# Two-block model kernel: first weight block in columns, time-step product in column strips, first decays of the delta layer ahead of its gate, and that layer's end by halves of the heads

## The reference, cut to what matters

```python
# first block: SSD mixer, then a mixture of experts, then a norm
proj = rmsnorm(x, norm_mix) @ w_in            # 1024 x (z, xbc, dt, sc_b, sc_c, sc_v)
dt = softplus(dt_raw + dt_bias)               # dt_raw: 16 columns of proj
...
# second block: layers fox0, gla, gdn (the delta layer), fox1
q, k, v = split(silu(causal_conv(qkv, conv_w)))
gc = cumsum(g, per chunk of tokens)
decay = exp(gc[i] - gc[j]) where i >= j
tri = strict_lower((k*beta) @ k.T * decay) + eye
u, w = solve(tri, v*beta), solve(tri, k*beta*exp(gc))
# per chunk: v_new = u - w @ state; o = q_dec @ state + qk @ v_new
# state = state*dec + k_dec.T @ v_new
return (rms_norm(o) * silu(z)) @ w_out
```

## Time and profile before

| | |
|---|---|
| median of 3 runs | 1295.03 us (1293.96 to 1295.28) |
| the profiled execution's own time | 1292.94 us |
| its span in the trace | 1291.2 us |
| PE, DVE, ACT, POOL busy | 86%, 50%, 34%, 1% of the span |
| time-mean granted PE clock | 0.964 of full speed |

### The profile page before, as it was taken

One profiled execution on the slowest core, in us unless ns is written; L12 is line 12 of the kernel. 1 busy time (PEld: TensorE's weight loads), 2 busy tenths in 40 slices (PEclk: granted clock), 3 DMA queues, 4 the chain that ended last, 5 costly groups with the idle time before them and its releaser, 6 DMA issues.

```text
span 1291.2 us, 19652 instructions
## 1 busy us (share of the span) xinstructions
PE 1106.5 (86%) x8060; PEld 811.6 (63%) x8060; DVE 644.5 (50%) x1265; ACT 439.2 (34%) x691; POOL 8.0 (1%) x35
## 2 busy tenths in 40 slices
PE   8999899897676758585858999999999979899998
PEld 7999767543131314131414789887779869778897
DVE  6787578420101111020104767667567965656685
ACT  5554435100000000000003556536346653255563
POOL 1000000000000000000000000000000000000000
PEclk9999999999898989898989999999999989899999
DMA  8575345999999999999998974254324530056600
GB/s 299 144 260 196 131 157 196 398 409 409 409 409 410 409 410 410 410 409 410 410 410 296 289 223 155 106 196 143 118 94 168 183 79 4 1 130 172 235 19 33
DMA packets 120005, 314.66 MB, mean 244 GB/s; under 512 B 17139, under 2 KB 17386, under 8 KB 119674
## 3 DMA queue, kind: packets, MB, share of 16 engines
q1 hardware_dynamic: 116864, 310.78, 65.9%
q0 software_dynamic: 352, 2.11, 0.4%
q10 hardware_dynamic: 2714, 0.71, 0.3%
HBM read 312.52 MB, written 1.06 MB: 243 GB/s over the span
## 4 chain that ended last, share of the span: by engine, by line
PE 58%; DMA 28%; DVE 8%; ACT 3%; issue 2%; SPq 1%; DVEq 0%; ACTq 0%
DMA ring<-in_w_up 18%; DMA ring<-in_w_down 10%; PE bank L2250 7%; PE bank L2243 7%; PE bank L2247 7%; PE bank L2225 6%; PE bank L2229 6%; PE bank L2232 6%; PE bank L2540 3%; PE bank L2563 2%; DVE w_l L1202 1%; PE bank L2158 1%; DMA ring<-in_w_in 1%; PE bank L2646 1%; ACT w_h L673 1%
## 5 line engine op out<-in xcount | busy, mean ns | idle before, releaser
L1202 DVE TENSOR_TENSOR w_l<-ring,w_h 128x1024 fp32r<-128x1024 f32 x204 | 246.6, 1221 | 90.7 <-ACT w_h L673 89.0
L673 ACT ACTIVATE w_h<-ring 128x1024 fp32r<-128x1024 f32 x204 | 213.6, 1056 | 176.4 <-PE bank L2232 88.7
L2540 PE MATMUL bank<-ring,cm 128*32 128x512 f32 x880 | 137.1, 754 | 101.0 <-DMA ring<-in_w_gate 61.5
L2540 PEld LDWEIGHTS bank<-ring,cm 128*32 128x32 f32 x880 | 27.7, 124 | 208.6 <-issue 78.5
L2243 PE MATMUL bank<-w_h,hnT_h 128*128 128x512 f32 x480 | 135.6, 405 | 5.1 <-DVE cm L1829 1.9
L2250 PE MATMUL bank<-w_l,hnT_h 128*128 128x512 f32 x480 | 129.7, 392 | 5.5 <-DVE w_l L1202 5.5
L2247 PE MATMUL bank<-w_h,hnT_l 128*128 128x512 f32 x480 | 129.7, 392 | 0.0
L1676 DVE SCALAR_TENSOR_TENSOR cm<-cm,bank 128x512 f32<-128x512 f32 x8 | 5.5, 688 | 215.0 <-ACT cm L895 215.0
L2250 PEld LDWEIGHTS bank<-w_l,hnT_h 128*128 128x128 f32 x480 | 89.6, 188 | 27.4 <-DVE w_l L1202 8.5
L2247 PEld LDWEIGHTS bank<-w_h,hnT_l 128*128 128x128 f32 x480 | 90.6, 189 | 20.0 <-DVE hnT_l L1317 0.2
L2243 PEld LDWEIGHTS bank<-w_h,hnT_h 128*128 128x128 f32 x480 | 86.9, 190 | 25.2 <-issue 4.5
(11 more groups left out here) (442 smaller groups left out, 1354.9 us busy)
## 6 DMA issues: line engine op xcount, KB each, us to landing
ring<-in_w_down SPq DMA_DIRECT2D x62, 1024.0 KB, 15.9
ring<-in_w_gate SPq DMA_DIRECT2D x56, 1024.0 KB, 15.6
ring<-in_w_up SPq DMA_DIRECT2D x54, 1024.0 KB, 15.8
ring<-in_fox_w_in SPq DMA_DIRECT2D x32, 1024.0 KB, 11.3
ring<-in_w_in SPq DMA_DIRECT2D x22, 1024.0 KB, 9.6
ring<-in_gla_w_in SPq DMA_DIRECT2D x12, 1024.0 KB, 6.3
ring<-in_gdn_w_in SPq DMA_DIRECT2D x12, 1024.0 KB, 6.8
ring<-in_w_out SPq DMA_DIRECT2D x8, 1024.0 KB, 6.3
```

Of the source, the lines that this page charges most:

```text
L673: af(part(w_h, u, width), w, ACT.Copy).then_inc(s["high_ready"], 1)
L1202: v.tensor_tensor(part(w_l, u, width), w, part(w_h, u, width).bitcast(F32), ALU.subtract).then_inc(s["low_ready"], 1)
L2540: x = mm(bank[a][CAP * e:CAP * (e + 1), :], m_xg[:, 2 * b + r, CAP * e:CAP * (e + 1)], expert_of(w, e)[:, r * FF:(r + 1) * FF], start=(b = ...
```

## The change

- The first weight block is loaded as one DMA of columns 0 to 255 of all 1024 rows (1 MB, semaphore `columns_loaded`), then two DMAs for the other columns. Units 0 and 1 wait for the first alone.
- `norm_mix` is the first vector loaded, counts with x in `x_loaded`, and is transposed and copied by itself, ahead of x's transposes; the other vectors are transposed in `first_steps`, after unit 2. On ACT the squares of x stand after the high parts of units 0 and 1.
- The eight dt products go to four column strips of PE (two products in each), with the 16 weights doubled to 32 columns by a copy on POOL; DVE copies the four partial sums and one more product adds them, after unit 10 (`dt_parts`, `dt_sum`).
- In `gdn()` the first spread of gc goes to bank 3 and its product to bank 4, and stands on PE ahead of the last z unit. On ACT the first z block stands ahead of the last convolution's Silu, the two decays of chunk 0 ahead of the second z block and of that Silu, and three w_h units of the output weights are moved into the inversion. The same units' w_l move on DVE.
- The end of `gdn()` goes by halves of the heads on PE, DVE and ACT; PE gets 20 unread products between the first transposes, and units 0 and 1 of the output projection both stand ahead of the third transposes.

```diff
+            def put_first(w, col):
+                slot = slot_whole(0)
+                v = w[:, col:col + BLK].rearrange("(c p) n -> p c n", p=P)
+                sp.dma_start(slot[:, :, 0:2 * P], v[:, :, 0:2 * P]).then_inc(s["columns_loaded"], 16)
+                for h in (0, 1):
+                    sp.dma_start(slot[:, 4 * h:4 * h + 4, 2 * P:BLK], v[:, 4 * h:4 * h + 4, 2 * P:BLK]).then_inc(ready[0], 16)
...
+            pool.wait_ge(s["small_loaded"], 16 * N_EARLY)
+            nc.gpsimd.tensor_copy(w_dt[:, :, 1, :], w_dt[:, :, 0, :]).then_inc(s["consts_ready"], 1)
...
+                if k == 3:
+                    break
...
+                high(UNIT_BASE["gdn_out"] - 1)
                 token_z("gdn", 16, 0)
-                high(UNIT_BASE["gdn_out"] + PARTS - 1)
+                high(UNIT_BASE["gdn_out"])
                 act.wait_ge(s["gdn_col_step"], 1)
-                token_z("gdn", 16, 1)
                 af(tok[:, 4:6, 0:8], tok[:, 4:6, 0:8], ACT.Exp).then_inc(s["gdn_col_step"], 1)
-                high(UNIT_BASE["gdn_out"] + PARTS)
...
                 decay(0, 0)
                 decay(0, 1)
+                token_z("gdn", 16, 1)
+                act.wait_ge(s["lin_ready"], 3 + 4)
+                af(tf(12, 4), vtm[:, 0, :], ACT.Silu).then_inc(s["gdn_conv_done"], 1)
...
-            def small_full(dst, w):
+            def dt_parts():
 
                 for k in range(KD):
-                    x = mm(dst, w[:, k, :], hnT[:, k, :], start=(k == 0), stop=(k == KD - 1))
+                    strip = slice(32 * (k % 4), 32 * (k % 4) + 32)
+                    x = mm(bank[5][strip, 0:T], w_dt[:, k].rearrange("p a b -> p (a b)"), hnT[:, k, :],
+                           start=(k < 4), stop=(k >= 4), tile_position=(0, 32 * (k % 4)), skip_group_check=True)
                 x.then_inc(s["small_done"], 1)
+
+            def dt_sum():
+
+                pe.wait_ge(s["rows_step"], 1)
+                mm(bank[5][0:16, 0:T], every16[:], rows[:, 0], start=True, stop=True).then_inc(s["small_done"], 1)
...
+                def gdn_tail():
+
+                    out, gains = UNIT_BASE["gdn_out"], [VCOL["gdn_o_gain"]] * 2
+                    out_sums("gdn", 8, 0, (0,))
+                    held_keys(0)
+                    out_sums("gdn", 8, 0, (1,))
+                    out_roots(8, 0, 1.0 / P, None, (0,))
+                    held_keys(1)
+                    new_values(0)
+                    out_roots(8, 0, 1.0 / P, None, (1,))
+                    new_values(1)
+                    out_roots(8, 0, 1.0 / P, None, (2,))
+                    for p in (0, 1):
+                        out_gated(8, 16, 0, p)
+                    out_sums("gdn", 8, 1, (0,))
+                    out_roots(8, 1, 1.0 / P, slice(8, 12))
+                    for p in (0, 1):
+                        out_gated(8, 16, 1, p)
+                    turned_low("gdn", 0, gains)
+                    out_sums("gdn", 8, 1, (1,))
+                    turned_low("gdn", 1, gains)
+                    out_roots(8, 1, 1.0 / P, slice(12, 16))
+                    for p in (2, 3):
+                        for t in range(NT):
+                            out_gated(8, 16, t, p)
+                        turned_low("gdn", p, gains)
+                        low(out + PARTS + p - 2)
```

More of the change, by code:

```diff
@@ L251, in build @@
         heads = sb("heads", [P, 3, 2 * 16])
-        rows = sb("rows", [16, 4, T])
+        rows = sb("rows", [P, 4, T])
         fall = sb("fall", [P, T])
@@ L1120, in link, with inverse_root @@
                 dve.wait_ge(s["dve_chain"], n_link[0])
-            def inverse_root(dst, x, t, done=None):
-                link(v.tensor_scalar(dst.bitcast(I32), x.bitcast(I32), -0.5, RSQRT_SEED, ALU.mult, ALU.add))
-                for k in range(3):
+            def inverse_root(dst, x, t, done=None, rounds=range(3)):
+                if 0 in rounds:
+                    link(v.tensor_scalar(dst.bitcast(I32), x.bitcast(I32), -0.5, RSQRT_SEED, ALU.mult, ALU.add))
+                for k in rounds:
                     link(v.tensor_tensor(t, dst, dst, ALU.mult))
@@ L1256, in first_norm @@
                 dve.wait_ge(s["vec_turned"], 2)
+                v.tensor_copy(vec[:, KD:NA], bank[3][:, KD:NA])
                 link(v.tensor_copy(vec[:, P:P + NB], bank[3][:, P:P + NB]))
@@ L2771, in gdn, with falls, last_block @@
                 project("gdn", 4, 5, lambda m: m == 3 and turn_sums("gdn_qk"))
[L2772 to L2774 removed]
+                def falls(c, hf):
+                    for j in range(4):
+                        x = tr(b4(g_fall[c][hf])[:, j, :], tok[:, c, 4 * hf + j:4 * hf + j + 1].to_broadcast([P, P]), ident[:])
+                    x.then_inc(s["gdn_fall"], 1)
+                def last_block(m):
+                    if m in (1, 2):
+                        spread("gdn_qk", 8, lambda i: [2 * (i % 4) + i // 4], [2 * m - 2, 2 * m - 1])
+                    if m == 2:
+                        pe.wait_ge(s["proj_copied"], PROJ_BASE["gdn"] + 10)
+                        falls(0, 0)
+                project("gdn", 5, 6, last_block)
                 def turn_values(c, hf):
+                    pe.wait_ge(s["gdn_conv_done"], 3 + hf)
                     if c:
@@ L2793, in blocks @@
                     return a.rearrange("p (h d) -> p h d", d=P)
-                def falls(c, hf):
-                    for j in range(4):
-                        x = tr(b4(g_fall[hf])[:, j, :], tok[:, c, 4 * hf + j:4 * hf + j + 1].to_broadcast([P, P]), ident[:])
-                    x.then_inc(s["gdn_fall"], 1)
                 def products(c, hf):
```

193 lines of the change are left out of this document (110 added, 83 removed).

## The result

The changed kernel takes 1288.42 us (median of 5 runs, 1286.89 to 1290.37) against 1295.03 (1293.96 to 1295.38). The ratio is 0.995, with a 95% interval from 0.9937 to 0.9964: 6.6 us faster, where 13.5 were forecast. The time lies 0.1 us inside the slow end of the range (1281.5, range 1277.5 to 1288.5), which is no credit to the mechanism: the range was that wide for rivals that did not come as written. Its profiled execution took 1288.80 us (span 1287.1), 4.1 less than that of the kernel before. A join is the step behind the last power that binds the two 64x64 inverses of each head together; there is one for each of the two chunks.

A forecast was written before the change was run, and what follows sets the result against it. DMA was taken as busy throughout only in the experts; work saved ahead moves their stream, work saved behind moves the end. Gains 2.8+2.1+6.1+2.5 = 13.5 us gave a median of 1281.5, range 1277.5 to 1288.5.

The forecast's parts named there:

- the clock's share of the head: Delta layer's head: 0.6 us taken off 6.7 for one slow PE stretch possibly falling on the powers; lower bound 3.5.
- PEclk of 0.5 within the inversion: Sign that the forecast is wrong: PE at half clock within the delta layer's inversion; no size given.
- First block, 2.8: Kernel start: first 1 MB lands at 9.3, so the root's spread begins 2.8 us earlier; bounds 0 and 3.1.
- Time step, 2.1: dt products: four strips and an added sum replace 3.56 us of PE, saving 2.1; bounds loss 0.45, gain 2.3.
- That what the front saves moves the whole stream of the experts: Ahead of the experts: work saved lets their loads start earlier and moves their whole stream; 2.8 and 2.1 us.
- rival 2: Experts: their DMA-bound stream swallows what the front saves, only 8.6 us of gain remain, 1286.4 us; chance 8%.
- Head, 6.1: Delta layer's head: halves 7.1 us earlier, copy of the first power 6.1 earlier; bounds 3.5 and 7.1.
- End, 2.5: Delta layer's end: work by halves of heads starts the output projection's unit 3 2.5 us earlier; bounds 1 and 3.5.
- Rival 3: Delta head: each added table switch costs another 1.28, or slow stretch hits powers twice; 2.6 us, 1284.1; chance 15%.
- Rival 4: Delta layer: the inversion stays at 1.2 GHz, some 28 us more, 1309.5 us; chance 3%.

The follow-up runs named there:

- e5: The changed kernel itself, run again for a second trace: 1287.50 us, 0.9921 of the kernel before.
- e3: Kernel before with only the delta layer's head changed: 1291.14 us, 0.9964 of the kernel before.
- e7: Changed kernel plus unread products ahead of the experts (14 more at the start, 16 between the sums of squares, 6 before the gather): 1287.59 us, 0.9918 of before.
- e10: Changed kernel plus 5 unread products ahead of the first join and 5 ahead of the first corner: 1285.70 us, 0.9915 of the kernel before.
- e12: Changed kernel plus only 16 unread products between the two sums of squares at 133 us: 1288.28 us, 0.9939 of the kernel before.
- e6: Changed kernel plus unread products in the delta layer (20 before halves, 24 before second power, 5 before first join, 5 before first corner): 1283.38 us, 0.9895 of before.
- e1: Kernel before with only the first block's change: 1292.29 us, 0.9995 of the kernel before.
- e11: e6 (18 products, not 24) plus early table load, 16 products between the sums, and ACT's first w_h moved behind the second power's copies: 1281.32 us, 0.9881 of before.
- e8: Changed kernel plus the unread products of e6 and e7 and a small activation moving the first table load earlier: 1282.79 us, 0.9888 of the kernel before.
- e2: Kernel before with only the time step's four strips: 1294.08 us, 0.9998 of the kernel before.
- e13: e9 with its 38 unread products moved ahead of PE's wait for the convolution: 1292.28 us, 0.9969 of the kernel before.
- e9: Kernel before plus unread products in the delta layer (38 before first spread, 22 before halves, 8 before second power, 5 and 5 at joins): 1295.99 us, 1.0002.
- e14: e11 plus 17 unread products around the first transposes of the gated linear attention's output: 1282.82 us, 0.9900 of the kernel before.
- e4: Kernel before with only the delta layer's end changed: 1293.82 us, 0.9993 of the kernel before.

## Why the prediction was wrong, by its steps

**The step that failed** is the clock's share of the head: "I take off 0.6 because PE now pauses three times where it was slow anyway", with a lower bound of 3.5 for "the slow stretch on two steps", and a rival that priced half clock only as the whole inversion at 1.2 GHz. The runs put between them a middle that the text did not have: single stretches of about 1.5 us of loss, where PE has pauses or thin work, and at places that the account of the head never reached, since it ended at the copy of the first power. One of its own signs of being wrong came, "PEclk of 0.5 within the inversion". In the changed kernel's layer they cost 0.7 at the halves (in the changed kernel and e5; 0.2 or less in e3, e7, e10 and e12), 1.3 to 1.6 behind the 3.1 us pause ahead of the second power (in each of these six traces, all without unread products there: 34.1 to 34.4 us from the first power's copy to the first join's, against 32.8 to 32.9 with them), 1.8 at the joins and 1.7 behind them (in two of the five without products there). e6 takes all of it back. How much the joins matter shows between traces of the same layer: from the entry to the end it gains 7.3 and 7.4 us on the kernel before in e12 and e7, and 3.4 and 3.5 in the changed kernel and e5, where 8.6 were forecast.

- *First block, 2.8.* 1.3 in the profiled pair, which has half clock at 13 to 16 us; 1.8 to 1.9 in e1, e5 and e6, which have none there. Two sizes were off. The table load of 1.28 us was not counted: it left the shade of x's landing. And the first columns landed at 9.5 to 9.9, not 9.3. (The text's own account, 20.89 - 17.9, gives 3.0 and not 2.8.) With the load moved (e11) the spread stands at 18.06, the predicted place. The last small load that POOL's copy needs was to come at most 0.6 later and comes 1.6 later (ACT had it at 35.59 instead of 34.02); that held PE in e8 alone, for 0.9.
- *Time step, 2.1.* Mechanism right, strips 1.1 and sum 0.6 by their rows; 1.7 to 1.8 at the second sum of squares (115.1 us behind the spread instead of 116.8, 115.0 in e2). No gain in time is seen for it alone.
- *That what the front saves moves the whole stream of the experts.* Right: rival 2 is out. What was lost, was lost ahead of them: 1.6 behind the sums of squares, 1.5 at the gather.
- *Head, 6.1.* Halves 7.3 earlier (7.1 forecast), first power's copy 6.7 (6.7 before the 0.6). The arithmetic of ACT's chain held, table loads included: each 1.28, the z at 1047.00 right behind the load of 1045.70. The drain of some 1.38 us per switch that the Trainium skill, "ScalarE: Activation LUTs", section What ACT_TABLE_LOAD costs, adds is in no row. But the sum set a new path at full clock against an old one in which 2.8 us were half clock. Full against full the head is worth 4.6. That the first power's 6.7 and e3's 5.9 came out as forecast rests on this old half clock, which the prediction had seen at the halves but not set apart.
- *End, 2.5.* The first copies of the turned output stand 2.5 earlier against the second join's copy where the joins are at full clock (20.40 in e6, 22.86 before). Then the two open transposes cost 0.93 each, as the text had it, and 1.0 of the gain goes: 1.5 stays. The text had that price and still kept 2.5 at unit 3; 1.9 was left there (unit 3 comes 12.4 us behind the first copies, 11.8 before), and the unit behind it lost 0.4 more.
- *Sum.* By the marks, with the clock held: 1.9 + 1.8 + 4.6 + 1.3 = 9.6 (5.9 - 4.6 = 1.3 for the end), and by the ratios e6 and e13 are about that apart, though the time step's 1.8 was not seen in a time of its own. Timed without unread products: 6.6. So of the 13.5 some 4 were terms of the wrong size and some 3 the clock; the marks carry the first of these, while the second, a difference of two times, lies within their error of some 4 and is an estimate. What the clock cost the changed kernel alone is surer: 4.1 us by e5 and e6. Rival 3 was half right: the table switches cost nothing beyond their 1.28, but slow stretches on the inversion were the mechanism, 4.8 us behind the first power's copy in the profiled run where it had 2.6. Rival 4, the whole inversion at half, did not happen.

## What to carry to other kernels

A step that is taken out of PE's path often leaves a pause or thin work where PE used to be busy, and the products behind it may run at 1.2 GHz: price each new pause at up to 1.9 us, and fill it with unread products while its length is known to cover them (in this kernel 54 small products were worth 4 us, put ahead of the waits; behind a wait they lay on the path, e9 and e14). Read a duration of the kernel before together with its PEclk before using it as a base. And judge changes of a few us by several executions, and by times behind a common mark: with the same work up to there, the first expert product came at 242.60, 243.19 and 245.62 in three kernels.

## What the runs showed of the hardware

- The same work fell to 1.2 GHz in one execution and not in another. Ahead of the changed kernel's slow joins, and ahead of the same joins in e3, which stayed at full clock, PE was equally busy, with 51 and 50 products. First the changed kernel's stretch there, then e3's and the one behind it:

```profile
1088.20:1091.50 3.30, 2.44 (x51) 2.21 (x48) 3.24 (x7) 0.59 (x1) 0.00 (x0) 1.00 0.00 0
```

```profile
1092.90:1096.20 3.30, 2.44 (x50) 2.23 (x49) 3.25 (x6) 0.59 (x1) 0.00 (x0) 1.00 0.00 0
1096.20:1103.00 6.80, 5.69 (x89) 5.19 (x84) 5.00 (x9) 1.37 (x3) 0.00 (x0) 1.00 0.02 4
```

  The changed kernel's next 10.3 us ran at 0.50, though PE was busy for 9.91 of them: once low, being busy on these products did not bring the clock back at once. The changed kernel fell there in both of its traces and e4, with the old head, in its one; e3, e7 and e12 did not. What sets it is open.
- The Trainium skill, "TensorE: Matmul & The Clock Gate", section HAM oscillation, tells such falls for PE's waits on DMA and advises to arrange the work so that PE stays busy. In the changed kernel's trace PE waits for no DMA in this layer; its waits are for ACT and DVE (3.1 us and 2.5 us the longest), and in e6, with them filled, the granted clock is 1.00 (2.4 GHz) from the halves to the joins.
- The first table load came only when the activation behind it was released: at 7.28, when PE had turned x, and not at 5.5, when ACT was free. A one-column activation ahead of the wait moved it to 5.79 (e8).
- Half-clock stretches added up evenly: the passage through the gated linear attention takes 256.3 to 256.6, 257.9 to 258.3, 259.3 to 259.4 or 261.0 to 261.1 us with none, one, two or three half-clock stretches in it.
